# Four small reorderings in a chain of eight transformer stages on one core

## What is computed

```
for i in 0, 1:                                  # first model
    mod = silu(c) @ ada_w[i] + ada_b[i]          # adaLN: shift, scale, gate for each sublayer
    h = h + 0.5*gate*rmsnorm(ffn(modulate(rmsnorm(h))))
    u = modulate(rmsnorm(h))
    y = differential_attention(u) if i == 0 else neighbourhood_attention(u)
    h = h + gate*rmsnorm(y)                      # i == 1: only the 256 latent tokens from here on
    h = h + 0.5*gate*rmsnorm(ffn(modulate(rmsnorm(h))))
for l in 0, 1:                                  # second model, "hybrid" layers
    p = rmsnorm(h) @ w_in                        # 16 column blocks
    y = concat(mla(p), gated_delta_net(p), moba(p))
    h = h + y @ w_out
return rmsnorm(h)
```

## Time and profile before

| | us |
|---|---|
| median of 3 runs | 2404.34 (2403.10 to 2405.17) |
| the profiled execution, its own time | 2404.16 |
| its span (first to last instruction) | 2402.3 |
| PE busy | 2309.5 (96%) |
| DVE busy | 1231.6 (51%) |
| ACT busy | 1002.9 (42%) |
| granted TensorE clock, mean | 0.986 of full speed |

### The profile page before, as it was taken

One profiled execution on the slowest core, in us unless ns is written; L12 is line 12 of the kernel. 1 busy time (PEld: TensorE's weight loads), 2 busy tenths in 40 slices (PEclk: granted clock), 3 DMA queues, 4 the chain that ended last, 5 costly groups with the idle time before them and its releaser, 6 DMA issues.

```text
span 2402.3 us, 40992 instructions
## 1 busy us (share of the span) xinstructions
PE 2309.5 (96%) x15234; PEld 1972.7 (82%) x15234; DVE 1231.6 (51%) x1714; ACT 1002.9 (42%) x1457; POOL 33.5 (1%) x35
## 2 busy tenths in 40 slices
PE   6999999999999999999999999999889989999998
PEld 5888888787777888888788888777789988988897
DVE  4322235765666332336532235745564577856765
ACT  4322224544455322225422234534554456345534
POOL 0000000000000000000000000000000000000000
PEclk9999999999989999999999999999989999999999
DMA  9663655312124544645332425422345644214321
GB/s 319 190 183 94 177 164 169 116 61 70 37 88 126 172 140 125 188 153 148 88 96 81 120 75 171 127 69 75 102 132 170 181 147 135 71 54 146 93 71 53
DMA packets 399015, 298.76 MB, mean 124 GB/s; under 512 B 12958, under 2 KB 360868, under 8 KB 398756
## 3 DMA queue, kind: packets, MB, share of 16 engines
q1 hardware_dynamic: 365322, 231.64, 33.4%
q10 hardware_dynamic: 33562, 65.35, 8.0%
HBM read 295.90 MB, written 1.06 MB: 124 GB/s over the span
## 4 chain that ended last, share of the span: by engine, by line
PE 78%; DVE 12%; ACT 4%; issue 3%; DMA 2%; SPq 1%; DVEq 0%; POOL 0%; ACTq 0%; POOLq 0%
PE banks L1045 22%; PE banks L1046 22%; PE banks L1047 22%; DVE wl L2411 3%; PE banks L870 2%; PE banks L1318 2%; ACT wh L1784 1%; DVE uR L2360 1%; DVE yT L2530 1%; PE banks L1180 1%; PE banks L1142 1%; DVE hT L2535 1%; DMA wraw<-in_ffn_w_in 1%; DMA big<-in_ada_w 1%; PE banks L1276 1%
## 5 line engine op out<-in xcount | busy, mean ns | idle before, releaser
L1045 PE MATMUL banks<-uR,wh 128*128 128x512 f32 (+1 forms) x2368 | 829.5, 350 | 22.7 <-DVE uR L2360 15.8
L1046 PE MATMUL banks<-uR,wh 128*128 128x512 f32 (+1 forms) x2368 | 814.3, 344 | 0.0
L1047 PE MATMUL banks<-uR,wl 128*128 128x512 f32 (+1 forms) x2368 | 813.8, 344 | 0.0
L2411 DVE TENSOR_TENSOR wl<-wraw,wh 128x2048 fp32r<-128x2048 f32 (+3 forms) x204 | 428.4, 2100 | 397.5 <-ACTq L1713 392.8
L1784 ACT ACTIVATE wh<-wraw 128x2048 fp32r<-128x2048 f32 (+4 forms) x208 | 366.8, 1764 | 470.0 <-PE banks L1047 413.9
L1045 PEld LDWEIGHTS banks<-uR,wh 128*128 128x128 f32 x2368 | 452.1, 191 | 94.3 <-issue 24.0
L1047 PEld LDWEIGHTS banks<-uR,wl 128*128 128x128 f32 x2368 | 452.0, 191 | 52.5
L1046 PEld LDWEIGHTS banks<-uR,wh 128*128 128x128 f32 x2368 | 452.5, 191 | 49.1 <-issue 0.5
L1045 PE MATMUL banks<-gR,wh 128*128 128x512 f32 (+1 forms) x704 | 256.6, 365 | 1.6 <-DVEq L2287 1.4
L1046 PE MATMUL banks<-gR,wh 128*128 128x512 f32 (+1 forms) x704 | 255.2, 363 | 0.0
L1047 PE MATMUL banks<-gR,wl 128*128 128x512 f32 (+1 forms) x704 | 255.2, 363 | 0.0
(11 more groups left out here) (333 smaller groups left out, 2369.3 us busy)
## 6 DMA issues: line engine op xcount, KB each, us to landing
wraw<-in_ffn_w_in SPq DMA_DIRECT2D x176, 512.0 KB, 5.1
ada_buf<-in_ada_w ACTq DMA_DIRECT2D x26, 2048.0 KB, 8.8
wraw<-in_w_in SPq DMA_DIRECT2D x56, 512.0 KB, 4.6
wraw<-in_ffn_w_out SPq DMA_DIRECT2D x64, 384.0 KB, 4.1
wraw<-in_ffn_w_out SPq DMA_DIRECT2D x64, 320.0 KB, 3.8
wraw<-in_da_w_in SPq DMA_DIRECT2D x24, 512.0 KB, 4.5
wraw<-in_na_w_in SPq DMA_DIRECT2D x24, 512.0 KB, 4.5
big<-in_ada_w SPq DMA_DIRECT2D x4, 2048.0 KB, 15.1
```

Of the source, the lines that this page charges most:

```text
L1045: mm(o, a[0], b[0], start=first, stop=False)
L1046: mm(o, a[0], b[1], start=False, stop=False)
L1047: return mm(o, a[1], b[0], start=False, stop=last)
L2411: do(V.tensor_tensor(wl[:, s, 0:n], wraw[:, s, 0:n], wh[:, s, 0:n].bitcast(F32), ALU.subtract), w_lo)
```

## The change

It has four parts; no instruction is added or removed.

1. In `na` the two transfers of the `ada_w` piece are issued at k = 5, behind that k's lead, no longer at k = 2. (For `da` the call stays at k = 2.)
2. In both attention loops on DVE the split that stood at the end of a step i = 1, 3 or 7 stands in the next step, behind that step's row maximum and scaling.
3. In the hybrid entry loop PE does unit 2 together with units 0 and 1 only for k = 0 to 3; its chunks 4 to 7 come behind the loop.
4. In `HY_DVE` the token `Ga` moves from ahead of `Sc.1.1 St.0` to behind them.

```diff
-            ... Di.1.0 Re.6 Sc.1.0 Ga Sc.1.1 St.0 Re.7
+            ... Di.1.0 Re.6 Sc.1.0 Sc.1.1 St.0 Ga Re.7
...
+        def split_unit(g, i):
+
+            return i in (1, 3) or i == 7 and g < 3
...
@@ PE, hybrid, first block
-                            ins = together([o[:, 0:SEQ] for o in psum[0:3]], (w[n], w[late]), lambda k: both(u2, k, slice(CTX, T)),
-                                           [u0 + k + 1 for k in range(DC)])
-                            ins[1].then_inc(hw_full, 1)
+
+                            def unit(k, c_):
+                                return product_step(psum[c_][:, 0:SEQ], both(w[late if c_ == 2 else n], k, slice(c_ % 2 * P, c_ % 2 * P + P)),
+                                                    both(u2, k, slice(CTX, T)), k == 0, k == DC - 1)
+
+                            for k in range(DC):
+                                pe.wait_ge(u_ready, u0 + k + 1)
+                                for c_ in range(3 if k < DC // 2 else 2):
+                                    ins = unit(k, c_)
+                            ins.then_inc(hw_full, 1)
+                            for k in range(DC // 2, DC):
+                                unit(k, 2)
...
@@ ACT, end of da and na
-                        if k == 2:
-                            fill_load(st, [0])
                         if k % 2 == 1 and k < DC - 1:
                             lead_next()
+                        if k == (5 if st == "na" else 2):
+                            fill_load(st, [0])
...
@@ DVE, da_heads, behind the scaling of item n
+                    if n > DA_STEPS[0] and split_unit(*da_unit(n - 1)):
+                        rest_next()
...
@@ DVE, da_heads, end of the step
-                        if i in (1, 3) or i == 7 and g < 3:
-                            rest_next()
...
@@ DVE, na_heads, behind the scaling
+                    if m - 1 > -7 and split_unit(*da_unit(m - 1)):
+                        rest_next()
...
@@ DVE, na_heads, end of the step
-                        elif i in (1, 3) or i == 7 and g < 3:
-                            rest_next()
```

More of the change, by code:

```diff
@@ L517, in build @@
         HY_DVE = [tok for tok, _ in steps("""
-            Re.0 C.5 Re.1 C.7 Re.2 C.6 Re.3 St.1 Re.4 Di.1.1 C.4 Re.5 C.3 Di.1.0 Re.6 Sc.1.0 Ga Sc.1.1 St.0 Re.7
+            Re.0 C.5 Re.1 C.7 Re.2 C.6 Re.3 St.1 Re.4 Di.1.1 C.4 Re.5 C.3 Di.1.0 Re.6 Sc.1.0 Sc.1.1 St.0 Ga Re.7
             Di.0.0 Gb Di.0.1 Sc.0.0 Cu Cb.1 Cb.0 Ms Re.8 Md.1 Md.0 KK.0 Me.1 Sc.0.1 TL.0 Xa.0 Re.9 Lm.1.0 Xt.0 QK.0
```

## The result

| | before | after |
|---|---|---|
| median | 2403.72 us (2402.57 to 2405.17, 4 runs) | 2383.62 us (2383.10 to 2386.44, 4 runs) |
| profiled execution, its own time | 2404.16 | 2384.12 |
| its span | 2402.3 | 2382.3 |
| PE busy, granted clock | 2309.5, 0.986 | 2300.7, 0.988 |

The interval alone allows a gain of 15.4 to 23.8 us, so the miss is better read from the traces than from the medians. Every part did what it was meant to do. So the question is not what went wrong in the kernel, but which terms of the sum were too small.

A forecast was written before the change was run, and what follows sets the result against it. PE was taken as the bound (78% of the last-ending chain, busy 96%), so only its idle time or lowered clock could be won. 6.0 + 1.2 + 3.9 + 2.1 + 2.6 = 15.8 us off 2404.16 gave 2388.4; range 2385.5 to 2395.

The forecast's parts named there:

- Split behind the scaling, `na`: Loop of `na`: DVE's maximum and scaling fall into its idle time, so six PE waits go; 6.0 us, bounds 0 and 6.0.
- The rival of ACT taking over the waits: In `na` PE meets ACT's copy (L1258) instead and every gain there is lost: 2394.4 us; chance 0.12.
- `da`: Maximum ahead of the split brings ACT's copy earlier, so two PE waits of 0.59 us go; 1.2 us, bounds 0 and 1.2.
- Transfers: End of `na`: piece issued behind the lead of k = 5, so PE's column sums start earlier; 3.9 us, bounds 3.5 and 4.3.
- the round of the DMA engines between the queues: DMA engines alternate packets between queues, so the stretch moves to the next weight transfer, 9.96 us if like the first.
- The clock's rival: End of `na`: the shorter wait keeps PE's clock up, winning 1.0 us at the sums, up to 0.5 behind: 2387.0; chance 0.12.
- Entry loop: Both hybrid layers: PE signals earlier, so its waits at `W.6.0` go; 2.1 us together, bounds 1.0 and 2.2.
- Gates: Both hybrid layers: `Sc.1.1` and `St.0` fill DVE's idle time before `Ga`; 1.3 us each, 2.6 together, lower bound 1.85 or 0.6.

The follow-up runs named there:

- the loops alone: The kernel before with the split moved in both attention loops and nothing else: 2394.06 us against 2403.94, ratio 0.9957.
- the entry loop alone: The kernel before with only the third unit's chunks 4 to 7 behind the hybrid entry loop: 2402.55 us, ratio 0.9991.

## Why the prediction was wrong, step by step

Two steps failed. The sum priced each removed wait at the idle time in its row and took that as the upper bound, "above, 6.0" in `na` and 1.2 in `da`; the waits gave 7.9 and 1.7. And it priced the gates of `hy0` by DVE's 1.3 us alone; 1.9 came, 0.5 of it from the clock. Another 1.0 us came in stretches that had no term. Not all of a row is a finding: over the profiles that have the part, the end of `na` with `ffn11` won 2.7 to 5.0 us.

- **Split behind the scaling, `na`: mechanism right, term too small by 1.9 us.** The sum took six waits at their row's value, 6.0. Of the 7.9 measured, 0.3 is a seventh wait (DVE, 0.31 us at 1587.33) that the sum left out, and 1.6 is what the row doesn't show at the seven waits, some 0.2 each. The rival of ACT taking over the waits didn't come: L1262 stands at 2.1 us as before.
- **`da`: the same error, 1.7 for 1.2.** Two waits of 0.59 us were worth 0.83 each.
- **Transfers: the term was right, one step of the argument was not.** The sums started 3.87 us earlier for the forecast 3.9, and the piece was in time (it landed at 1734.7, PE wanted it at 1739.5). The 7.2 us from the lead to the sums is not what the prediction's own figures give (6.4 and the issues' 0.95 make 7.35); 7.18 was measured, so this was in part luck. The wait before the sums was 1.52 us for the 0.9 forecast, since the prediction left out what PE wins at k = 5. It also said, by the round of the DMA engines between the queues, that the next weight transfer would be the stretched one, near 10 us. It took 5.2: it had a head start of 2 us on the piece, where the stretched one of before was issued 1.7 us behind it. The traces show a long transfer only for the blocks issued behind the piece (8.7 and 9.96 us before, up to 9.4 with the piece behind k = 6). The clock's rival is half true: the sums ran at full clock, and DVE took most of the gain.
- **Entry loop: right**, 0.85 and 1.1 for 1.0 and 1.1. In `hy0` a signal of DVE is next late, which the prediction hadn't named.
- **Gates: mechanism right, `hy0` too small by 0.6 us.** The sum priced a wait of 2.04 us shortened to 0.65 by DVE's 1.3 us alone. The fall of the clock behind the long wait was in the trace of before, and the prediction had not looked behind that wait. In `hy1` the argument held that the whole 1.3 would come though PE's wait there was 0.55: 1.4 came. Its reason was another than PE running late by itself: the clock had been down before `Di.0.0`, which hid the rest of the wait.

```profile
2236.00:2238.00 2.00, 2.00 (x12) 2.00 (x11) 1.33 (x5) 1.91 (x5) 0.28 (x1) 0.50 0.00 0
2238.00:2240.00 2.00, 2.00 (x14) 2.00 (x13) 2.00 (x1) 1.28 (x3) 1.36 (x1) 0.65 0.00 0
```

  (These are slices of the kernel before.) With the loops alone, where the clock was still up at that point, PE waited the full time in `hy1` too:

```profile
2231.59 0.70 PE L1386 MATMUL banks<-cst 128*128 128x512 f32 x1 [2.03 <-DVEq L2291]
```

- **Start of `hy1`, 0.7 us, and start of the program, 0.3: in no term.** The entry loop of `hy1` begins at half clock, and how soon the clock comes back differed: over the thirteen profiles of changed kernels the offset there grew by anything from 0 to 1.0 us. The seven profiles with the moved gates and no added operation lie at 0.5 to 1.0, the three with an added operation at 0 to 0.4, the three without the moved gates at 0 to 0.5. The Trainium skill, page "TensorE: Matmul & The Clock Gate", section "What's actually happening", says that the window of the clock gate runs freely; that fits a return at varying places, but no run here separates chance from an effect of the shifted start, so this stays open.
- **The range.** It reached 2.9 us below the forecast, 1.5 of it for the clock, and gave the terms no error of their own toward the fast side. The errors of the loops (2.4 us together) and of the gates had one sign, and added up.

## What to carry to other kernels

Where nothing else takes a wait's place, its removal gives more than its row shows: add the overlap of a matmul with the next (start to start against its length, 0.16 us for 256 columns here), and look at the granted clock ahead of and behind every wait that the change shortens. Where several waits of one kind go, this error has one sign and grows with their number. The row is no lower bound, though: in the entry of `hy0` a wait of 1.09 us gave 0.85, since another signal was next late. And when an engine sits idle for an input, whatever of its later work has its inputs already can be put ahead: it took one operation of 1.23 us out of the way to remove six waits of 1 us. Before a difference of 1 us is put down to a change, see whether the clock fell somewhere in one profile and not in the other.

## What the runs showed of the hardware that was not expected

In `hy0` a wait of PE of 1.38 us left the granted clock at 1.00, one of 2.04 to 2.10 us was followed by 0.5 to 0.6 in all five profiles that had it, and the fall cost 0.5 us beyond the wait. It is no rule: in `hy1` the same wait of 2.03 us was followed by a fall in one profile and by full clock in another, and near the end of `na` (1711 us of the kernel before) the clock fell in 3 of 14 profiles, though PE's waits in the 15 us ahead of it are the same in all.

A stretch at half clock that ends in a wait for another engine costs nothing: in `hy1` the kernel before had the fall ahead of `Di.0.0` and waited 0.55 us, the entry loop alone had no fall and waited 2.03, and PE's offset between the two changed by 0.01 us over the place.

Of a weight block and the 2 MB piece in flight together it was the block that grew, and only where it was issued second: it took 5.2 us when issued 2 us ahead of the piece and 9.96 when issued 1.7 us behind it, while the piece's larger part took 7.9 and 7.8.
